# Key, value and query tiles in rows of their own, head sums and rotations one weight slab later

## The chip, the cores and the metric

One core of one Trainium2 chip runs the kernel. The metric is device microseconds of one execution. Before the change the median of three runs is 2245.8 us (2245.16 to 2245.82).

## The reference, cut to what matters

A two-layer backbone works on 512 latent tokens and 256 context tokens of width 1024. Each layer has a token-mixing part with three branches (attention, pooling, convolution) and a gated feed-forward part. The change touches only how the attention inputs are made. In short:

```python
ux = hx @ w_in[i]                                # queries, keys, values, pool, conv, gates
q = rope(rmsnorm(heads(ux[..., :512]), q_norm))  # 8 heads of 64
k = rope(rmsnorm(heads(ux[..., 512:640]), k_norm))   # 2 heads of 64, context rows without rope
v = ux[..., 640:768]
p = softmax(q * 64**-0.5 @ k.T); o = p @ v
```

In layer 0 context and latent tokens (768 columns) have queries; in layer 1 only the latent ones (512 columns), while keys and values need all 768.

## The kernel before, in words

All activations are held transposed, features on the 128 partitions and tokens along the row. A weight matrix comes in slabs of up to eight 128x128 blocks; `gemm` (L529) multiplies one slab into a PSUM bank pair, in three passes (high x high, low part of x, low part of w), since every operand is split into an fp32r high part and remainder. SP loads a slab into one of two raw buffers (L382), ScalarE rounds it (`rounds`, L893) into one of four ring places, GpSimd subtracts to get the low part (`split_run`, L425), and TensorE uses it. SP loads a slab only when the split two slabs earlier has ended. `result_of(s)` on ScalarE first rounds all slabs up to s + 3, and then waits for slab s's GEMM. Every engine has its instructions in one fixed order written out by hand; each waits on counting semaphores.

`A[0]` and `A[1]` are two PSUM places of 1024 columns for GEMM results, `B` a third for transposes and spreads, `OD` a fourth for rotations, with head sums beside it. `t1`, `t2`, `t3` are three rows of 800 columns in SBUF. `acc` is an accumulator of eight rows that isn't used while queries, keys and values are made.

The stage in question has six tiles of 128 features: k, v, q0, q1, q2, q3. Key and value are one `gemm_pair` (L555) that follows the normalised input block by block; each query tile is one slab. For a k or q tile:
- ScalarE squares the PSUM tile into `t1` (L1023) and copies it, scaled by the norm's gain, into `t2` (L1026), which frees the PSUM place;
- TensorE sums the squares per head and token (`head_sums`, L600, products of two columns) and multiplies `t2` by a rotation matrix into OD (`sums`, L583);
- VectorE multiplies by sine into `t3` (L1543), `t2` by cosine (L1545), and adds (L1547);
- for k alone, VectorE's variance (L1299, L1300), ScalarE's root (L940) and TensorE's spread of it over the features (L613, 24 products) come first, and then VectorE multiplies (L1552);
- ScalarE copies the tile as fp32r high part (L1036 for k, four half-tile copies; L1041 for q, two), and VectorE writes the remainders (L1559, L1564), the last of which is the event `tile`.

For v, ScalarE copies the tile into `t1` (L1016), TensorE transposes it in six products (L680), ScalarE copies the high part (L1020) and VectorE makes the remainder (L1534).

As all tiles share `t1` and `t2`, ScalarE waits for `tile` of the one before, ahead of each eviction:

```python
result_of(...)                       # L1012
if prev: act.wait_ge(*seen("tile", ly, prev))
```

On TensorE the GEMM of tile n comes before the products of tile n - 1 (`finish`). Behind q3 come the GEMM of the convolution's gate, the products of q3, and the GEMM of its value branch. ScalarE takes the root of all q variances (L940), then the tanh of the gate (L1050, with an ACT table load of its own), and VectorE multiplies it with the value branch (L1575). Only then are both places free for the attention scores (L726): VectorE takes the row maximum (L1585) and its negated, scaled copy (L1589), ScalarE the exponential (L1075), VectorE the division (L1599), TensorE the transposes (L736) and products with v (L757). Attention is the stage that follows, 80 units in both layers together.

Of the kernel before, what the change touches and what calls it, by code (L numbers as in the profile page):

```python
# [27 lines left out]
ACT = mybir.ActivationFunctionType  # L28
# [3 lines left out]
P = 128  # L32
# [88 lines left out]
def build(nc, io, known):  # L121
# [33 lines left out]
    with ctx:  # L155
# [115 lines left out]
        def at(w, c0, c1):  # L271
            return w[:, 256 + c0:256 + c1]
# [236 lines left out]
        def _(pe):  # L509
# [146 lines left out]
            for ly in range(LAYERS):  # L656
# [12 lines left out]
                    spread(0, "pre1", ly, "pre1")  # L669


                tiles = ["k", "v", "q0", "q1", "q2", "q3"]

                def finish(n):
                    c = full if n in "kv" else cols
                    if n == "v":
                        take("B", "vt", ly)
                        pe.wait_ge(*seen("vcopy", ly))
                        for k in range(6):
                            ins = nc.tensor.transpose(at(B, k * P, (k + 1) * P), t1[:, k * P:(k + 1) * P], ident)  # L680
                        ins.then_inc(*pe_done.up("vt", ly))
                    else:

                        pe.wait_ge(*seen("tsq", ly, n))
                        if "OD" in last_use:
                            pe.wait_ge(*seen("free", *last_use["OD"]))
                        col, per = (TOK["k"], 2) if n == "k" else (TOK["q"] + 2 * int(n[1]), HEADS)
                        head_sums(t1, c[0][0], col, per).then_inc(*pe_done.up("stat", ly, n))
                        sums(rot, t_cols(t2), c, ("free", "gemm", ly, n), "rot", ly, n, w="OD")
                        if n == "k":  # L690
                            spread(0, "k", ly, "k", heads=KV)

                for n, name in enumerate(tiles):
                    w = n % 2
                    take(w, "gemm", ly, name)
                    if name == "v":
                        s = s0 + S_KV
                        gemm_pair(A, [(s, s + 1, 4), (s + 2, s + 3, 4)], (hh, hl), high_ready, low_ready, full)
# [182 lines left out]
        def _(act):  # L881
# [113 lines left out]
            for ly in range(LAYERS):  # L995
# [10 lines left out]
                h_high(ly, "pre1", 0, 0)  # L1006


                prev = None
                for n, name in enumerate(["k", "v", "q0", "q1", "q2", "q3"]):  # L1010
                    w, l0 = A[n % 2], (0 if name in "kv" else lo)
                    result_of(s0 + (S_KV + 2, S_KV + 3, S_Q, S_Q + 1, S_Q + 2, S_Q + 3)[n])  # L1012
                    if prev:
                        act.wait_ge(*seen("tile", ly, prev))
                    if name == "v":
                        nc.scalar.activation(t1[:, 0:T], at(w, 0, T), ACT.Copy).then_inc(  # L1016
                            *act_out.up("free", "gemm", ly, name))
                        noted[("vcopy", ly)] = noted[("free", "gemm", ly, name)]
                        act.wait_ge(*seen("vt", ly))
                        nc.scalar.activation(vh[:].rearrange("p a b -> p (a b)"), at(B, 0, T),  # L1020
                                             ACT.Copy).then_inc(*act_hi.up("vh", ly))
                    else:
                        nc.scalar.activation(t1[:, l0:T], at(w, l0, T), ACT.Square).then_inc(  # L1023
                            *act_tmp.up("tsq", ly, name))
                        gcol = V_KN if name == "k" else V_QN
                        nc.scalar.activation(t2[:, l0:T], at(w, l0, T), ACT.Copy,  # L1026
                                             scale=vec[:, ly, gcol:gcol + 1]).then_inc(
                            *act_out.up("free", "gemm", ly, name))
                        if name == "k":
                            root("k", 2 * TT, ly, "k")  # L1030
                        act.wait_ge(*seen("roped", ly, name))
                        if name == "k":

                            for kv in range(KV):
                                for p in range(2):
                                    ins = nc.scalar.activation(kk[64 * p:64 * p + 64, 2 * kv, :],  # L1036
                                                               t2[64 * kv:64 * kv + 64, 0:T], ACT.Copy)
                        else:
                            j = int(name[1])
                            for p in range(2):  # L1040
                                ins = nc.scalar.activation(qs[64 * p:64 * p + 64, 2 * j + p, l0:T],  # L1041
                                                           t2[64 * p:64 * p + 64, l0:T], ACT.Copy)
                        ins.then_inc(*act_hi.up("hi", ly, name))
                    prev = name
# [241 lines left out]
        def _(dve):  # L1286
# [235 lines left out]
            for ly in range(LAYERS):  # L1522
# [4 lines left out]
                    normalise(ly, "pre1", 0, 0, 0)  # L1527


                for n, name in enumerate(["k", "v", "q0", "q1", "q2", "q3"]):  # L1530
                    l0 = 0 if name in "kv" else lo
                    if name == "v":
                        dve.wait_ge(*seen("vh", ly))
                        v.tensor_tensor(vl[:].rearrange("p a b -> p (a b)"), at(B, 0, T),  # L1534
                                        vh[:].rearrange("p a b -> p (a b)"), ALU.subtract).then_inc(
                            *dve_lo.up("free", "vt", ly))
                        noted[("tile", ly, "v")] = noted[("free", "vt", ly)]
                        continue
# [4 lines left out]
                    v.tensor_tensor(t3[:, l0:T], at(OD, l0, T), sin[:, l0:T], ALU.mult).then_inc(  # L1543
                        *dve_out.up("free", "rot", ly, name))
                    link(v.tensor_tensor(t2[:, l0:T], t2[:, l0:T], cos[:, l0:T], ALU.mult), dve_tmp)  # L1545
                    dve.wait_ge(*dve_out.ago())
                    link(v.tensor_tensor(t2[:, l0:T], t2[:, l0:T], t3[:, l0:T], ALU.add), dve_tmp,  # L1547
                         *(() if name == "k" else ("roped", ly, name)))
                    if name == "k":

                        dve.wait_ge(*seen("spread", ly, name))
                        link(v.tensor_tensor(t2[:, 0:T], t2[:, 0:T], at(B, 0, T), ALU.mult), dve_tmp,  # L1552
                             "roped", ly, name)
                        noted[("free", "spread", ly, name)] = noted[("roped", ly, name)]
                    dve.wait_ge(*seen("hi", ly, name))
                    for a in range(2):
                        if name == "k":
                            for p in range(2):
                                ins = v.tensor_tensor(kk[64 * p:64 * p + 64, 2 * a + 1, :], t2[64 * a:64 * a + 64, 0:T],  # L1559
                                                      kk[64 * a:64 * a + 64, 2 * a, :], ALU.subtract)  # L1560
                                ins.then_inc(*(dve_lo.up("tile", ly, name) if a and p else dve_lo.up()))
                        else:
                            j = int(name[1])
                            ins = v.tensor_tensor(qs[64 - 64 * a:128 - 64 * a, 2 * j + a, l0:T],  # L1564
                                                  t2[64 * a:64 * a + 64, l0:T],
                                                  qs[64 * a:64 * a + 64, 2 * j + a, l0:T], ALU.subtract)
                            ins.then_inc(*(dve_lo.up("tile", ly, name) if a else dve_lo.up()))

                noted[("stat", ly, "q")] = noted[("stat", ly, "q3")]
                t0 = lo // P  # L1570
                variance("q", t0 * HEADS, (TT - t0) * HEADS, HD, ly, "q")

                dve.wait_ge(*seen("free", "cgate", ly, 0))
                dve.wait_ge(used, s0 + S_CONV + 2)
# [404 lines left out]
```

## Time and profile before

| | |
|---|---|
| median of 3 runs | 2245.8 us (2245.16 to 2245.82) |
| the profiled execution, its own time | 2242.06 us |
| its span in the trace | 2240.3 us |
| busy: TensorE, VectorE, ScalarE, GpSimd | 2134.7, 1337.7, 794.9, 783.3 us |
| mean granted TensorE clock | 0.982 of full |
| instructions | 27947 |

The span runs from the first to the last instruction of the profiled execution; its own time is a little longer, and is compared with the other runs. Busy shares are means over stages with different limits, so a stage is read from its own stretch. Lines such as L529 are those of a helper that all GEMMs share. A number in brackets at the end of a row of the timeline is the idle time before it and what ended it. Granted clock 1.00 is 2.4 GHz, 0.50 is 1.2 GHz.

### The profile page before, as it was taken

The page shows a single profiled execution, that of the slowest core. Times are in us where ns is not written, and L with a number is a line of the kernel's source. Part 1 is how long each engine was busy: PE and PEld are TensorE (multiplying, and loading weights), DVE is VectorE, ACT ScalarE, POOL GpSimd, SP SyncE. Part 2 cuts the span into 40 slices and gives each one's busy share as a digit, 9 for nine tenths or more (in the row PEclk, how much of TensorE's full clock was granted, in tenths as well). Part 3 has the DMA queues.
Part 4 walks back from the last instruction along what each step waited for, and adds up shares of the span by engine and source line. Part 5 has one row for each costly group of instructions (what it writes and reads, how often), then busy time and mean ns, then how long its engine had stood idle before and what let it go on. Part 6 is the DMA issues. An engine that isn't in the chain of part 4 may idle for free.

```text
span 2240.3 us, 27947 instructions
## 1 busy us (share of the span) xinstructions
PE 2134.7 (95%) x11302; PEld 1807.4 (81%) x11302; DVE 1337.7 (60%) x1812; ACT 794.9 (35%) x1154; POOL 783.3 (35%) x359
## 2 busy tenths in 40 slices
PE   6889899999999999999999987899999999999997
PEld 6777788888888888888888876677867877888885
DVE  6459899856774587847616674798954353101113
ACT  2446711142324522223212344572234344222223
POOL 3220023232334433423323345103444555444442
PEclk9999999999999999999999989999999999999998
DMA  7110012123344134534323221102222332323321
GB/s 295 38 47 1 1 52 70 43 88 112 105 159 151 58 119 134 187 101 135 105 85 111 94 95 66 48 1 66 88 78 90 108 123 82 97 94 95 94 85 66
DMA packets 63200, 205.24 MB, mean 92 GB/s; under 512 B 7136, under 2 KB 8288, under 8 KB 62816
## 3 DMA queue, kind: packets, MB, share of 16 engines
q1 hardware_dynamic: 57744, 190.87, 26.2%
q10 hardware_dynamic: 5328, 12.59, 1.5%
q8 instruction: 90, 1.47, 0.3%
q14 instruction: 38, 0.31, 0.0%
HBM read 197.79 MB, written 5.64 MB: 91 GB/s over the span
## 4 chain that ended last, share of the span: by engine, by line
PE 78%; DVE 17%; ACT 2%; issue 1%; DMA 1%; POOL 1%; ACTq 0%; DVEq 0%
PE ps L529 70%; DVE conv_acc L1624 3%; DVE ps L1624 2%; DVE unit_stats L1585 2%; PE ps L555 2%; DVE pt1l L1605 1%; DVE probs L1599 1%; DVE pt0l L1605 1%; PE ps L736 1%; PE ps L592 1%; PE ps L573 1%; PE ps L613 1%; PE ps L583 1%; PE ps L757 1%; PE ps L600 1%
## 5 line engine op out<-in xcount | busy, mean ns | idle before, releaser
L425 POOL TENSOR_TENSOR w_l<-w_raw,w_h 128x1024 fp32r<-128x1024 f32 (+3 forms) x296 | 683.7, 2314 | 1305.7 <-ACT w_h L893 1305.4
L529 PE MATMUL ps<-h_h,w_h 128*128 128x512 f32 (+1 forms) x1296 | 430.4, 372 | 5.9 <-ACT t L1145 4.2
L529 PE MATMUL ps<-h_l,w_h 128*128 128x512 f32 (+1 forms) x1296 | 426.1, 369 | 0.0
L529 PE MATMUL ps<-h_h,w_l 128*128 128x512 f32 (+1 forms) x1296 | 425.3, 368 | 0.0
L893 ACT ACTIVATE w_h<-w_raw 128x1024 fp32r<-128x1024 f32 (+3 forms) x296 | 280.5, 950 | 212.2 <-PE ps L529 148.6
L529 PEld LDWEIGHTS ps<-h_h,w_h 128*128 128x128 f32 x1296 | 244.8, 190 | 55.8 <-ACT t L1145 6.6
L529 PEld LDWEIGHTS ps<-h_h,w_l 128*128 128x128 f32 x1296 | 245.7, 190 | 43.6
L529 PEld LDWEIGHTS ps<-h_l,w_h 128*128 128x128 f32 x1296 | 245.4, 189 | 42.9 <-issue 1.2
L1485 DVE CUSTOM_DVE_ANT_0 ps<-ada_raw,c_row 128x1024 f32<-128x1024 f32 x160 | 268.4, 1677 | 9.1 <-DMA ada_raw<-in_ada 4.1
L529 PE MATMUL ps<-f_h,w_h 128*128 128x258 f32 (+1 forms) x672 | 173.1, 339 | 0.9 <-DVE t L1810 0.9
L529 PE MATMUL ps<-f_h,w_l 128*128 128x258 f32 (+1 forms) x672 | 173.5, 340 | 0.0
L529 PE MATMUL ps<-f_l,w_h 128*128 128x258 f32 (+1 forms) x672 | 172.4, 338 | 0.0
L529 PE MATMUL ps<-mid_h,w_l 128*128 128x512 f32 (+1 forms) x528 | 160.7, 359 | 0.0
L529 PE MATMUL ps<-mid_h,w_h 128*128 128x512 f32 (+1 forms) x528 | 160.0, 357 | 0.1
L529 PE MATMUL ps<-mid_l,w_h 128*128 128x512 f32 (+1 forms) x528 | 159.1, 355 | 0.0
L1624 DVE SCALAR_TENSOR_TENSOR ps<-conv_in,vec,ps 128x512 f32<-128x512 f32 (+1 forms) x180 | 143.8, 845 | 2.1
L529 PEld LDWEIGHTS ps<-f_h,w_h 128*128 128x128 f32 x672 | 127.5, 190 | 16.1 <-DVE t L1810 1.2
L529 PEld LDWEIGHTS ps<-f_l,w_h 128*128 128x128 f32 x672 | 127.1, 189 | 14.6
L529 PEld LDWEIGHTS ps<-f_h,w_l 128*128 128x128 f32 x672 | 127.0, 189 | 14.6
L529 PEld LDWEIGHTS ps<-mid_h,w_h 128*128 128x128 f32 x528 | 99.4, 188 | 16.2 <-DVE acc L1835 0.4
L529 PEld LDWEIGHTS ps<-mid_l,w_h 128*128 128x128 f32 x528 | 99.2, 188 | 15.5
L529 PEld LDWEIGHTS ps<-mid_h,w_l 128*128 128x128 f32 x528 | 99.2, 188 | 14.7
(236 smaller groups left out, 3222.6 us busy)
## 6 DMA issues: line engine op xcount, KB each, us to landing
w_raw<-in_w SPq DMA_DIRECT2D x222, 512.0 KB, 3.6
ada_raw<-in_ada SPq DMA_DIRECT2D x80, 512.0 KB, 3.6
w_raw<-in_w SPq DMA_DIRECT2D x50, 256.0 KB, 3.2
ada_first<-in_ada SPq DMA_DIRECT2D x16, 512.0 KB, 6.7
w_raw<-in_w SPq DMA_DIRECT2D x16, 384.0 KB, 3.1
x<-in_x ACTq DMA_DIRECT2D x8, 384.0 KB, 17.6
x_again<-in_x ACTq DMA_DIRECT2D x8, 384.0 KB, 7.7
x_between<-x SPq DMA_DIRECT2D x8, 384.0 KB, 2.3
```

What stands on the lines that cost most here:

```text
L425: nc.gpsimd.tensor_tensor(wl[:, s % RING, 0:n], raw[:, s % RAW, 0:n], wh[:, s % RING, 0:n], ALU.subtract).then_inc(split, 1)
L529: ins = nc.tensor.matmul(at(out, c0, c1), w[:, s % RING, b * P:(b + 1) * P], m[:, kt, first + c0:first + c1], start=(kt == 0 and n == 0), ...
L555: ins = nc.tensor.matmul(at(out, c0, c1), w[:, s % RING, b * P:(b + 1) * P], m[:, k, first + c0:first + c1], start=(i == 0 and n == 0), st ...
L573: ins = nc.tensor.matmul(DD[:, 2 * k:2 * k + 2], ada_first[:, n % ADA_SLOTS, b * P:(b + 1) * P], silu_c[:, b, :], start=(b == 0), stop=(b ...
L583: ins = nc.tensor.matmul(at(B if w == "B" else OD, c0, c1), mat, src(c0, c1), start=True, stop=True)
L592: ins = nc.tensor.matmul(token_sum(kind, TOK[kind] + t, 1), src[:, t * P:(t + 1) * P], ones[:, 0:1], start=start and first, stop=stop and ...
L600: ins = nc.tensor.matmul(token_sum("q", c, 2), src[:, t * P:(t + 1) * P], blk[:, 0:P:HD], start=True, stop=True)
L893: nc.scalar.activation(wh[:, n % RING, 0:nb * P], raw[:, n % RAW, 0:nb * P], ACT.Copy).then_inc(*rounded.up())
L1485: link(v.tensor_tensor_reduce(out=scratch, in0=tile, in1=c_row[:, s, :], scale=1.0, scalar=0.0, op0=ALU.mult, op1=ALU.add, accum_out=mod[: ...
L1585: link(v.reduce_max(ust[:, 0, c:c + n], at(A[u % 2], 0, n * nk).rearrange("p (r k) -> p r k", k=nk), AX.X), dve_tmp)
L1605: v.tensor_tensor(key_rows(pl, us[u - 2]), by_key_tile(at(B, 0, nk * q_tiles(us[u - 2])), us[u - 2]), key_rows(ph, us[u - 2]), ALU.subtrac ...
L1624: return v.scalar_tensor_tensor(out=taps_of(ly, j), in0=src, scalar=w, in1=taps_of(ly, j), op0=ALU.mult, op1=ALU.add)
```

## The change

The tiles of key and query get rows of `acc` for squares, scaled copy and sine product (q1 uses `acc[:, 7]`, `t1`, `t2`), value one row. Key's result goes to `A[1]`, value's to `A[0]`. Value's copy out of PSUM moves from ScalarE to VectorE, ahead of key's rotation. On TensorE key's products come after q0's GEMM and its spread after q1's; the products of q0 to q2 come a slab later than before, those of q3 keep their place. ScalarE's evictions wait only for the tile whose rows they reuse. The q variance comes before the last rotation, and root and tanh come before q3's copies. The diff, cut to its core (the bodies of the rotation and remainders are as before, with the new rows):

```diff
+        tile_bank = {"k": 1, "v": 0, "q0": 0, "q1": 1, "q2": 0, "q3": 1}
+        tile_rows = {"k": (acc[:, 0], acc[:, 1], acc[:, 2]), "v": (acc[:, 3],), "q0": (acc[:, 4], acc[:, 5], acc[:, 6]),
+                     "q1": (acc[:, 7], t1, t2), "q2": (acc[:, 4], acc[:, 5], acc[:, 6]),
+                     "q3": (acc[:, 7], acc[:, 0], acc[:, 1])}
...
@@ TensorE
-                for n, name in enumerate(tiles):
-                    w = n % 2
-                    take(w, "gemm", ly, name)
-                    if name == "v":
...
-                    elif name != "k":
-                        gemm(A[w], [(s0 + S_Q + n - 2, 8)], hh, hl, cols)
-                    if n:
-                        finish(tiles[n - 1])
...
+                gemm_pair((A[1], A[0]), [(s, s + 1, 4), (s + 2, s + 3, 4)], (hh, hl), high_ready, low_ready, full)
+                q_slab("q0")
+                head_products("k")
+                take("B", "vt", ly)
+                pe.wait_ge(*seen("free", "gemm", ly, "v"))
+                for k in range(6):
+                    ins = nc.tensor.transpose(at(B, k * P, (k + 1) * P), tile_rows["v"][0][:, k * P:(k + 1) * P], ident)
+                ins.then_inc(*pe_done.up("vt", ly))
+                q_slab("q1")
+                spread(0, "k", ly, "k", heads=KV)
+                head_products("q0")
+                q_slab("q2")
+                head_products("q1")
+                q_slab("q3")
+                head_products("q2")
                 take(0, "cgate", ly, 0)
                 gemm(A[0], [(s0 + S_CONV, 8)], hh, hl, cols)
-                finish(tiles[-1])
+                head_products("q3")
...
@@ ScalarE
+                result_of(s0 + S_KV + 3)
+                evict("k", V_KN, 0)
+                result_of(s0 + S_Q)
+                evict("q0", V_QN, lo)
+                root("k", 2 * TT, ly, "k")
+                act.wait_ge(*seen("vt", ly))
...
+                result_of(s0 + S_Q + 1)
+                evict("q1", V_QN, lo)
+                act.wait_ge(*seen("roped", ly, "k"))
...
+                q_high("q0")
+                result_of(s0 + S_Q + 2)
+                act.wait_ge(*seen("tile", ly, "q0"))
+                evict("q2", V_QN, lo)
+                q_high("q1")
+                result_of(s0 + S_Q + 3)
+                act.wait_ge(*seen("tile", ly, "k"))
+                act.wait_ge(*seen("tile", ly, "q1"))
+                evict("q3", V_QN, lo)
+                q_high("q2")
+                result_of(s0 + S_CONV)
                 root("q", HEADS * TT, ly, "q", scale=1.0 / HD)
-
-                result_of(s0 + S_CONV)
-                act.wait_ge(*seen("stat", ly, "q3"))
                 nc.scalar.activation(t1[:, lo:T], at(A[0], lo, T), ACT.Tanh, scale=0.5).then_inc(
                     *act_out.up("free", "cgate", ly, 0))
+                q_high("q3")
                 result_of(s0 + S_CONV + 1)
...
@@ VectorE
+                    if name == "q3":
+                        variance("q", lo // P * HEADS, (TT - lo // P) * HEADS, HD, ly, "q")
...
+                dve.wait_ge(used, s0 + S_KV + 4)
+                v.tensor_copy(tile_rows["v"][0][:, 0:T], at(A[0], 0, T)).then_inc(*dve_out.up("free", "gemm", ly, "v"))
+                turn("k", 0)
+                dve.wait_ge(*seen("vh", ly))
...
+                dve.wait_ge(*seen("spread", ly, "k"))
...
+                turn("q0", lo)
+                dve.wait_ge(*seen("hi", ly, "k"))
...
+                q_low("q0")
+                for name in ("q1", "q2", "q3"):
+                    turn(name, lo)
+                    q_low(name)
```

## Rows read from the trace of the kernel before

**Rows 1.** The page: span, chain by engine, weight loads (count, size, us to landing).
```profile
span 2240.3 us, 27947 instructions
...
PE 78%; DVE 17%; ACT 2%; issue 1%; DMA 1%; POOL 1%; ACTq 0%; DVEq 0%
...
w_raw<-in_w SPq DMA_DIRECT2D x222, 512.0 KB, 3.6
```

**Rows 2.** Chain of waits, layer 0 (start us, us, what).
```profile
84.95 2.84 PE ps L613 x24
...
94.35 3.05 DVE k_split L1559
...
100.28 9.96 PE ps L529 x48
...
112.87 8.43 PE ps L529 x48
...
154.52 1.28 ACT L1050
...
158.67 1.36 DVE unit_stats L1589
...
160.14 1.09 ACT probs L1075 x2
```

**Rows 3.** Timeline of TensorE, layer 0 (start us, us, engine, line, operation, idle before).
```profile
78.67 1.57 PE L555 MATMUL ps<-h_l,w_h 128*128 128x256 f32 x8
...
99.44 0.85 PE L680 MATMUL ps<-const,t 128*128 128x128 f32 x6 [2.03 <-ACT t L1016]
...
156.68 2.29 PE L726 MATMUL ps<-k_split,q_split 128*128 128x256 f32 x8 [2.22 <-ACT t L1050]
```

**Rows 4.** Chain of waits, layer 1.
```profile
1391.34 0.79 PE ps L600 x8
...
1393.09 5.58 PE ps L529 x24
...
1427.99 1.09 ACT probs L1075 x2
```

**Rows 5.** Timeline of TensorE, layer 1.
```profile
1363.19 1.57 PE L555 MATMUL ps<-h_l,w_h 128*128 128x256 f32 x8
...
1369.07 1.53 PE L613 MATMUL ps<-const,token_rs 128*64 128x128 f32 x24 [0.86 <-ACT token_rs L940]
...
1383.05 1.51 PE L680 MATMUL ps<-const,t 128*128 128x128 f32 x6 [6.67 <-ACT t L1016]
...
1424.53 2.89 PE L726 MATMUL ps<-k_split,q_split 128*128 128x256 f32 x8 [2.95 <-ACT t L1050]
```

**Rows 6.** Windows of 1 us, layer 0: busy us by engine, then granted clock, DMA.
```profile
84.00:85.00 1.00, 0.14 (x3) 0.08 (x3) 0.81 (x3) 0.21 (x1) 0.00 (x0) 0.50 0.00 0
```

**Rows 7.** Timelines of VectorE, then ScalarE, both layers.
```profile
101.16 0.96 DVE L1534 TENSOR_TENSOR v_l<-ps,v_h 128x768 fp32r<-128x768 f32 x1 [2.77 <-ACT v_h L1020]
...
160.92 0.16 DVE L1589 SCALAR_TENSOR_TENSOR unit_stats<-unit_stats,token_rs 128x1 f32<-128x1 f32 x1
...
161.45 0.62 DVE L1599 TENSOR_SCALAR probs<-probs,unit_stats 128x768 f32<-128x768 f32 x1
...
1396.56 1.40 DVE L1564 TENSOR_TENSOR q_split<-t,q_split 64x512 fp32r<-64x512 f32 x2 [1.41 <-ACT q_split L1041]
...
88.87 3.41 ACT L1036 ACTIVATE k_split<-t 64x768 fp32r<-64x768 f32 x4 [4.07 <-DVE t L1552]
...
1398.05 0.60 ACT L1023 ACTIVATE t<-ps 128x512 f32<-128x512 f32 x1 [0.51 <-DVE q_split L1564]
```

**Rows 8.** Queue of SP, layer 1: weight loads (first issue, us, count).
```profile
1365.49 62.72 SPq L382 DMA_DIRECT2D w_raw<-in_w  x9
```

**Rows 9.** Timeline of GpSimd, layer 0.
```profile
93.44 3.14 POOL L425 TENSOR_TENSOR w_l<-w_raw,w_h 128x1024 fp32r<-128x1024 f32 x1 [14.58 <-ACT w_h L893]
...
157.65 2.36 POOL L425 TENSOR_TENSOR w_l<-w_raw,w_h 128x1024 fp32r<-128x1024 f32 x1 [0.73 <-ACT w_h L893]
```

More of the change, by code:

```diff
@@ L669, in _ @@
                     spread(0, "pre1", ly, "pre1")
[L672 to L691, printed above, removed]
@@ L693, in _, with q_slab @@
[L693 to L702 removed]
+                def q_slab(n):
+                    take(tile_bank[n], "gemm", ly, n)
+                    gemm(A[tile_bank[n]], [(s0 + S_Q + int(n[1]), 8)], hh, hl, cols)
@@ new lines, in head_products @@
+                def head_products(n):
+                    c = full if n == "k" else cols
+                    square, scaled, _ = tile_rows[n]
+                    pe.wait_ge(*seen("tsq", ly, n))
+                    if "OD" in last_use:
+                        pe.wait_ge(*seen("free", *last_use["OD"]))
+                    col, per = (TOK["k"], 2) if n == "k" else (TOK["q"] + 2 * int(n[1]), HEADS)
+                    head_sums(square, c[0][0], col, per).then_inc(*pe_done.up("stat", ly, n))
+                    sums(rot, t_cols(scaled), c, ("free", "gemm", ly, n), "rot", ly, n, w="OD")
@@ L1006, in _ @@
                 h_high(ly, "pre1", 0, 0)
[L1009 to L1044, printed above, removed]
@@ new lines, in evict @@
+                def evict(name, gain_col, l0):
+                    square, scaled, _ = tile_rows[name]
+                    w = A[tile_bank[name]]
+                    nc.scalar.activation(square[:, l0:T], at(w, l0, T), ACT.Square).then_inc(*act_tmp.up("tsq", ly, name))
+                    nc.scalar.activation(scaled[:, l0:T], at(w, l0, T), ACT.Copy,
+                                         scale=vec[:, ly, gain_col:gain_col + 1]).then_inc(
+                        *act_out.up("free", "gemm", ly, name))
@@ new lines, in q_high @@
+                def q_high(name):
+                    act.wait_ge(*seen("roped", ly, name))
+                    j, scaled = int(name[1]), tile_rows[name][1]
+                    for p in range(2):
+                        ins = nc.scalar.activation(qs[64 * p:64 * p + 64, 2 * j + p, lo:T],
+                                                   scaled[64 * p:64 * p + 64, lo:T], ACT.Copy)
+                    ins.then_inc(*act_hi.up("hi", ly, name))
+                result_of(s0 + S_KV + 3)
+                evict("k", V_KN, 0)
@@ L1527, in _, with turn @@
                     normalise(ly, "pre1", 0, 0, 0)
[L1530 to L1538, printed above, removed]
+                def turn(name, l0):
+                    _, scaled, other = tile_rows[name]
                     dve.wait_ge(*seen("rot", ly, name))
@@ L1546, in _, with q_low @@
                     dve.wait_ge(*dve_out.ago())
-                    link(v.tensor_tensor(t2[:, l0:T], t2[:, l0:T], t3[:, l0:T], ALU.add), dve_tmp,
+                    link(v.tensor_tensor(scaled[:, l0:T], scaled[:, l0:T], other[:, l0:T], ALU.add), dve_tmp,
                          *(() if name == "k" else ("roped", ly, name)))
[L1549 to L1554, printed above, removed]
+                def q_low(name):
@@ L1555, in _ @@
                     dve.wait_ge(*seen("hi", ly, name))
+                    j, scaled = int(name[1]), tile_rows[name][1]
                     for a in range(2):
[L1557 to L1567, printed above, removed]
@@ new lines, in _ @@
+                dve.wait_ge(*seen("spread", ly, "k"))
+                scaled = tile_rows["k"][1]
+                link(v.tensor_tensor(scaled[:, 0:T], scaled[:, 0:T], at(B, 0, T), ALU.mult), dve_tmp, "roped", ly, "k")
+                noted[("free", "spread", ly, "k")] = noted[("roped", ly, "k")]
+                turn("q0", lo)
+                dve.wait_ge(*seen("hi", ly, "k"))
+                for a in range(2):
+                    for p in range(2):
+                        ins = v.tensor_tensor(kk[64 * p:64 * p + 64, 2 * a + 1, :], scaled[64 * a:64 * a + 64, 0:T],
+                                              kk[64 * a:64 * a + 64, 2 * a, :], ALU.subtract)
+                        ins.then_inc(*(dve_lo.up("tile", ly, "k") if a and p else dve_lo.up()))
```

23 lines of the change are left out of this document (19 added, 4 removed).

## The prediction

> **What bounds the kernel now.** I read the page first. TensorE holds 78% of the chain that ended last, of a span of 2240.3 us [rows 1]. So the end moves when TensorE's idle or slow stretches go, and not when another engine does less. The diff touches one stage in each layer, from the end of the key/value GEMM pair to the first softmax exponential, so I followed the chain of waits through both copies of it, then TensorE's timeline there for its gaps.
>
> In layer 0 the pair ends at 78.67 + 1.57 = 80.24 [rows 3]. After it come key's head sums and rotation, the wait for key's root, and key's spread, which ends at 84.95 + 2.84 = 87.79 [rows 2]. Only then does query slab q0 start. After q0 TensorE idles 2.03 us until value's copy L1016 [rows 3]: ScalarE may write `t1` only when VectorE is through with key's tile, and VectorE's third key remainder took 3.05 us [rows 2]. Then the q slabs run back to back: a slab takes 8.43 us, and the slab at 100.28, which came behind that idle, 9.96; the products after it last from 110.24 to 112.87, 2.63 us [rows 2]. The value-branch GEMM ends at 156.68 - 2.22 = 154.46; the 2.22 us are the wait for the gate's tanh [rows 3], whose table load starts only at 154.52. The first exponential starts at 160.14 [rows 2].
>
> Layer 1 has the same shape with 512 columns: the pair ends at 1364.76, TensorE idles 6.67 us ahead of value's transposes and 2.95 ahead of the scores, so the last GEMM ends at 1421.58 [rows 5]; a slab takes 5.58, its products 1393.09 - 1391.34 = 1.75, and the exponential starts at 1427.99 [rows 4]. The extra time on a slab behind a gap is the clock: granted 0.50 (1.2 GHz) at 84 to 85 us, after head sums and rotations with short waits [rows 6], against full clock (2.4 GHz) in the steady slabs.
>
> **The change, part by part.**
>
> *Value's bank.* q0 now uses the bank of value, not of key. So it waits for value's PSUM-to-row copy, new on VectorE and ahead of key's rotation there. The trace has no such plain copy of 768 columns. The nearest are L1534 with a PSUM operand, 0.96 us, and L1599, SBUF to SBUF, 0.62 us [rows 7]. I take 0.96, since it reads PSUM, with 0.05 us on either side: 1.06 us in each layer. VectorE stands idle there, so nothing is queued behind it but key's rotation, which comes only after q0.
>
> *Key's products a slab later.* They no longer wait for an eviction: key's is done during q0's 8.43 or 5.58 us. They cost 2.63 us at full clock. Root and variance of key are hidden behind q1, so the spread has no wait and costs what it costs in layer 1, 1.53 us [rows 5], instead of 2.84 at the low clock. If that cover went, the waits of 0.86 us between products and spread would come back.
>
> *Value's copy and transposes.* The copy needs no tile of key any more, so the waits of 2.03 and 6.67 us go, and with them the slow slabs behind them. The transposes cost 0.85 [rows 3].
>
> *Weights.* Per slab, the rounding on ScalarE, the split on GpSimd and the load that SP issues are as before in number and order. Moved is the third rounding of the stage (slab S_KV+6), now ahead of key's eviction. In layer 1 its load is issued only when the split two slabs earlier ends, at 1365.49 [rows 8]; with the page's 3.6 us to landing [rows 1] it is there at 1369.1. Passes of 768 columns take 3.41 / 4 = 0.85 us by L1036 [rows 7], so one of 1024 some 1.1: it is rounded at 1370.2, and key's square and scaled copy end at 1371.0 and 1371.9. TensorE wants the first at 1364.8 + 1.06 + 5.58 = 1371.4 and the second after the head sums, so this costs nothing, by 0.4 us. In layer 0 the load was issued earlier and there is room.
>
> *Rows of their own.* Evictions no longer wait for the tile just before, but q2's still waits for the remainders of q0, which now stand behind all of key's. In layer 1, counted from the end of q1's GEMM: spread 1.53, multiply 0.96, key's four copies 3.41, its four remainders 3.84 (by L1534's 0.96 each), q0's two 1.40, q2's square 0.60, with one block by a split (2.1) 13.9 us [rows 7]. TensorE wants that square after spread, two products and two slabs: 1.53 + 2 x 1.75 + 2 x 5.58 = 16.2. So it costs nothing, by 2.3 us; in layer 0, with slabs of 8.43, there is more room. Later tiles take 1397.96 - 1393.09 = 4.9 us from rotation to last remainder [rows 4, 7] and 0.7 more to the end of the next square, 1398.65, and have two slabs for it.
>
> *Root and tanh ahead of copies.* Variance comes before the last rotation, root before the table load, tanh before q3's copies. The tanh ended 156.68 - 154.52 = 2.16 us after its table load began; with variance and root ahead (an estimate: at most as long again) that is 4.3 us beside a value-branch GEMM of 8.43 or 5.58. So the waits of 2.22 and 2.95 us go. What is late next is VectorE's gate product and the row maximum: in layer 0 158.67 - 156.68 = 1.99 us, then the negated maximum. That took 1.36 us [rows 2], since a GpSimd split ran until 160.01 [rows 9]; its next one takes 0.16 [rows 7]. The split now ends before it. With 0.05 and 0.11 us of issue the tail is 2.3 us in layer 0. In layer 1 the gate product is shorter, but the maximum needs the scores: half of the 2.29 us for two units [rows 3], 1.15, plus 1.0 for the maximum (half of 1.99), 0.16 and 0.11 gives 2.4.
>
> **The sum.** Layer 0, pair to last GEMM: 1.06 + 6 x 8.43 + 5 x 2.63 + 0.85 + 1.53 = 67.2, against 154.46 - 80.24 = 74.2: 7.0 less. Tail 2.3 against 5.7: 3.4 less. Layer 1: 1.06 + 6 x 5.58 + 2.63 + 4 x 1.75 + 0.85 + 1.53 = 46.6, against 56.8: 10.2 less. Tail 2.4 against 6.4: 4.0 less. Together 24.7 us (rounded terms add to 24.6). Attention starts that much earlier in each layer and is itself unchanged. The profiled execution took 2242.1 us (1.8 outside its span) and gives 2217.4; the median of the runs lies 3.7 above it, at 2245.8, so the forecast is 2221.1.
>
> **A rule against it.** The third key remainder started at 94.35 while a GpSimd split ran from 93.44 to 96.58; it ended at 97.40, so it did its 0.95 us after the split [rows 2, 9]. The gaps that the change removes ahead of value are partly this. In the new order other operations with both inputs in SBUF (rotation multiply and add, remainders) meet splits at new places; rival 1 prices that.
>
> The Trainium skill, in "SBUF — State Buffer", section "Who interferes with whom", says that a VectorE instruction with two SBUF inputs contends with a GpSimd one that reads SBUF, and the first to start holds the port for its whole length. By that rule, the trace agrees: 3.05 us for a 0.95 us instruction. Without it the sum is 2221.1, with it at the end of both stages rival 1's.
>
> **The rivals.**
> 1. *Blocked at the end (15%).* The split of the last slab before attention starts 1.1 us after q3's copies, about when the second of its two remainders does. Before, these started just ahead of the split. If the split is first, the remainder, gate product and maximum wait for it, up to 2.4 us [rows 9] a layer: 2225.9. Blocks further up eat the 2.3 us of slack in layer 1 before they cost TensorE anything. For: layer 1's remainders end within 0.2 us of its last GEMM. Against: the order on the two engines is the same as in the old steady slabs.
> 2. *The clock falls in thin stretches (12%).* Key's products and transposes now stand together (3.5 us), then spread and q0's products (4.2 us), and 1.06 us of idle comes ahead of q0. For: the 0.50 at 84 us. Against: layer 1's spread took 1.53 us behind the same products, so the clock stayed full there [rows 5], and so it did in the steady slabs of 8.43. A fall costs 9.96 - 8.43 = 1.5 us on a slab; at four places 6.1 us: 2227.2.
> 3. *Slower: the tile chain becomes the bound (3%).* Place: q2's eviction, which waits for q0's remainders behind key's, and each later one. It decides from 14.7 us per two slabs in layer 1 and 22.1 in layer 0. A tile's chain is 1.75 + 4.9 + 0.7 = 7.3 us in layer 1, some 11 in layer 0 (an estimate by the columns). If each of its five operations waited for a whole split of 3.14 us [rows 9], 23.0 and 26.7 would give 4.2 and 2.3 us more per slab, over six slabs 39 us, less the 24.7: 2260. Against: there is one split per slab, so five blocks per tile cannot be had.
> 4. *It does not arrive (4%).* If attention's first units wait for late tiles of q or for VectorE, only a fifth of it is left: near 2241, within 0.2% of 2245.8, about what a measurement of this kernel can tell from no change.
>
> **How the numbers follow.** My case has 66%. Its own range is 2217 to 2224: the copy at 0.62 and a shorter tail give a microsecond or two, the profile's lower time gives more, and lost slack takes up to 3. The high end adds rivals 1 and 2 together: 2221.1 + 4.8 + 6.1 = 2232. Low end 2216. Left out are rivals 3 and 4 and about 10% on the two sides. Faster by over 0.2% holds all but rivals 3 and 4: 93%; the same 4%; slower 3%.
>
> **What would show it.** TensorE's idle between pair and q0 near 1.1 us and none ahead of the transposes; spread 1.5 us in layer 0; granted clock full from pair to scores; no idle between last GEMM and scores; first exponentials near 149.7 and 1403 (1413.7 less layer 0's 10.4); first negated maximum 0.16 us. I am wrong if TensorE waits for ScalarE's square before a product, if the clock shows 0.50 between slabs, or if the last q remainder runs over 2 us.

## The result, and the profile after

The changed kernel takes 2218.6 us (median of four runs, 2217.3 to 2220.6) against 2245.8 (2245.2 to 2246.7) of the kernel before beside it: a ratio of 0.9879, 95% interval 0.9862 to 0.9896. Its profiled execution took 2219.4 us, with a span of 2217.6. The forecast was 2221.1, with 2216 to 2232 as its range.

One slip in what stands ahead of the prediction: the section on the change says that the products of q0 to q2 come a slab later than before. They don't; before, too, they stood behind the GEMM of the next query slab. Only key's products move (from ahead of q0's GEMM to behind it) and its spread (to behind q1's). The sum of the prediction counted them rightly.

The changed page: span, busy time of TensorE, and the share of each engine in the chain that ended last.

```profile
span 2217.6 us, 27943 instructions
...
PE 2129.1 (96%) x11302; PEld 1805.5 (81%) x11302; DVE 1340.1 (60%) x1814; ACT 793.2 (36%) x1152; POOL 784.1 (35%) x359
...
PE 78%; DVE 16%; ACT 2%; DMA 1%; issue 1%; POOL 1%; ACTq 0%; DVEq 0%; SPq 0%
```

Work is as before; the span is 22.7 us shorter. The chain of waits in layer 0 answers to [rows 2] (start us, us, what; L534 is the GEMM, L605 the head sums, L588 the rotation, L703 the transposes, L618 the spread):

```profile
80.61 0.97 DVE acc L1570
...
81.62 8.71 PE ps L534 x48
90.33 1.23 PE ps L605 x12
91.56 1.40 PE ps L588 x4
92.96 0.66 PE ps L703 x6
93.61 8.42 PE ps L534 x48
102.03 1.46 PE ps L618 x24
...
139.49 8.44 PE ps L534 x48
...
149.89 0.17 DVE unit_stats L1609
...
150.16 1.09 ACT probs L1089 x2
```

After the value copy L1570, everything down to the last GEMM is TensorE, one piece behind the other. The spread takes 1.46 us and the slab behind value's transposes 8.42; before they took 2.84 and 9.96 [rows 2]. The stage has no stretch at the lower clock.

Layer 1, the same view, answers to [rows 4]:

```profile
1355.08 0.97 DVE acc L1570
...
1356.09 5.85 PE ps L534 x24
...
1370.80 1.46 PE ps L618 x24
...
1396.22 5.59 PE ps L534 x24
...
1403.53 0.50 DVE unit_stats L1609
...
1404.14 1.09 ACT probs L1089 x2
```

**The measure used below** is the way from the end of the key/value pair to the start of the first exponential, read in each profile. It was 160.14 - 80.24 = 79.9 us in layer 0 and 63.2 in layer 1. It is 150.16 - 80.57 = 69.6 and 1404.14 - 1355.04 = 49.1. So the stage gives 10.3 + 14.1 = 24.4 us; the prediction said 24.7. For the changed kernel it repeats to 0.1 us: a second profile gave 69.6 and 49.1 again. The kernel before has one profile; its layer 0 held a fall of the clock behind the pair (granted 0.50 from 84 to 89 us); e9 below, without it, came out 2.8 us shorter than forecast. e2, which is the same up to its tail, shows that fall too, at the same place. Whole times do not repeat so well; the section on the clock has their spread.

### The profile page after: what moved, and what is told of

It is laid out like the page before. It is cut to its first block, busy times and chain, and to the rows that moved or that the text cites. A ratio compares the mean times of both kernels' runs of the same rounds, so it can differ in the third digit from the quotient of the medians.

```text
span 2217.6 us, 27943 instructions
## 1 busy us (share of the span) xinstructions
PE 2129.1 (96%) x11302; PEld 1805.5 (81%) x11302; DVE 1340.1 (60%) x1814; ACT 793.2 (36%) x1152; POOL 784.1 (35%) x359
## 4 chain that ended last, share of the span: by engine, by line
PE 78%; DVE 16%; ACT 2%; DMA 1%; issue 1%; POOL 1%; ACTq 0%; DVEq 0%; SPq 0%
PE ps L534 71%; DVE conv_acc L1644 3%; DVE ps L1644 2%; DVE unit_stats L1605 2%; PE ps L560 2%; DVE pt0l L1625 1%; DVE pt1l L1625 1%; DVE probs L1619 1%; PE ps L597 1%; PE ps L744 1%; PE ps L578 1%; DMA w_raw<-in_w 1%; PE ps L618 1%; PE ps L588 1%; POOL w_l L430 1%
## 5 line engine op out<-in xcount | busy, mean ns | idle before, releaser
L534 PE MATMUL ps<-h_h,w_h 128*128 128x512 f32 (+1 forms) x1296 | 427.9, 370 | 8.2 <-ACT t L1159 4.2
L534 PE MATMUL ps<-h_l,w_h 128*128 128x512 f32 (+1 forms) x1296 | 425.0, 368 | 0.0
L534 PE MATMUL ps<-h_h,w_l 128*128 128x512 f32 (+1 forms) x1296 | 424.6, 368 | 0.0
L534 PEld LDWEIGHTS ps<-h_h,w_h 128*128 128x128 f32 x1296 | 243.6, 189 | 58.4 <-ACT t L1159 6.6
L534 PEld LDWEIGHTS ps<-h_h,w_l 128*128 128x128 f32 x1296 | 244.7, 189 | 43.4
L534 PEld LDWEIGHTS ps<-h_l,w_h 128*128 128x128 f32 x1296 | 244.2, 188 | 42.1 <-issue 1.2
L534 PE MATMUL ps<-f_h,w_h 128*128 128x258 f32 (+1 forms) x672 | 173.1, 339 | 0.9 <-DVE t L1830 0.9
L534 PE MATMUL ps<-f_h,w_l 128*128 128x258 f32 (+1 forms) x672 | 173.5, 340 | 0.0
L534 PE MATMUL ps<-f_l,w_h 128*128 128x258 f32 (+1 forms) x672 | 172.4, 338 | 0.0
L534 PE MATMUL ps<-mid_h,w_l 128*128 128x512 f32 (+1 forms) x528 | 160.7, 359 | 0.0
L534 PE MATMUL ps<-mid_h,w_h 128*128 128x512 f32 (+1 forms) x528 | 160.0, 357 | 0.1
L534 PE MATMUL ps<-mid_l,w_h 128*128 128x512 f32 (+1 forms) x528 | 159.1, 355 | 0.0
L534 PEld LDWEIGHTS ps<-f_h,w_h 128*128 128x128 f32 x672 | 127.5, 190 | 16.2 <-DVE t L1830 1.2
L534 PEld LDWEIGHTS ps<-f_l,w_h 128*128 128x128 f32 x672 | 127.1, 189 | 14.7
L534 PEld LDWEIGHTS ps<-f_h,w_l 128*128 128x128 f32 x672 | 127.0, 189 | 14.6
L534 PEld LDWEIGHTS ps<-mid_h,w_h 128*128 128x128 f32 x528 | 99.4, 188 | 16.1 <-DVE acc L1855 0.4
L534 PEld LDWEIGHTS ps<-mid_l,w_h 128*128 128x128 f32 x528 | 99.3, 188 | 15.6
L534 PEld LDWEIGHTS ps<-mid_h,w_l 128*128 128x128 f32 x528 | 99.2, 188 | 14.7
```

The source lines that it names most:

```text
L534: ins = nc.tensor.matmul(at(out, c0, c1), w[:, s % RING, b * P:(b + 1) * P], m[:, kt, first + c0:first + c1], start=(kt == 0 and n == 0), ...
```

## The experiments

### The tail: e1 and e2

e1 puts the old order at the end of the stage back into the changed kernel, e2 puts the new one alone into the kernel before.

```diff
 e1, ScalarE (VectorE's variance goes behind q3's remainders)
+                q_high("q3")
+                root("q", HEADS * TT, ly, "q", scale=1.0 / HD)
                 result_of(s0 + S_CONV)
-                root("q", HEADS * TT, ly, "q", scale=1.0 / HD)
                 nc.scalar.activation(t1[:, lo:T], at(A[0], lo, T), ACT.Tanh, scale=0.5).then_inc(
                     *act_out.up("free", "cgate", ly, 0))
-                q_high("q3")
```

> The changed kernel with the old order at its end: q3's copies and remainders first, then variance, root, rounding and tanh. Theory (the chain root to tanh is on the path when it stands behind the copies, and hidden beside the value-branch GEMM when ahead): TensorE idles some 2.3 us ahead of the scores in layer 0 and 3.0 in layer 1, and the first negated maximum is blocked by a split again, so the first exponentials come 3.6 and 4.2 us later than in the changed kernel: about 7.8 us longer, near 2226.5. Rival (the tail is hidden anyway by VectorE's gate product and row maximum): under 2 us longer.

> The kernel before with this part alone: variance of q ahead of the last rotation, root and tanh ahead of q3's copies; rows and order of the rest as before. Theory (the parts are independent and add): 3.4 us less in layer 0; in layer 1 4.0 less, or 3.4 if a split blocks q3's rotation: 6.8 to 7.4 us below the kernel before, near 2238.7. Rival (the tail pays only once the earlier stalls are gone, since q3's remainders are late): under 3 us less.

e1 measured 73.0 and 53.2 us from pair to exponential: 3.4 and 4.1 more than the changed kernel, where 3.6 and 4.2 were expected. Its median is 2227.0 (2224.9 to 2228.0), and its ratio to the kernel before 0.9936, interval 0.9921 to 0.9951. e2 measured 76.5 and 59.6: 3.4 and 3.6 less than the kernel before. Its median is 2236.5 against 2241.2, 4.7 less, and its ratio 0.998, interval 0.9969 to 0.9992, which is 1.8 to 6.9 us: the whole time gives somewhat less than the stage. Read in the stage, the theory holds from both sides: the part is worth 7.0 to 7.5 us, with or without the rest of the change. The chain of waits of e1 in layer 1 shows where it sits:

```profile
1405.56 0.95 issue
1406.51 1.28 ACT L1064
...
1407.81 0.60 ACT t L1064
1408.41 0.04 issue
1408.46 0.98 PE ps L734 x4
...
1410.45 1.35 DVE unit_stats L1608
...
1411.91 1.09 ACT probs L1089 x2
```

The rounding (shown as 0.95 us of issue), the table load and the tanh all stand between copies and scores, and the negated maximum L1608 takes 1.35 us, where the next one takes 0.16: a split ran from 1409.43 to 1411.78.

### Value's row alone: e9

The transposes read the new row; every order stays.

```diff
-                    if prev:
+                    if prev and name != "v":
                         act.wait_ge(*seen("tile", ly, prev))
...
-                        nc.scalar.activation(t1[:, 0:T], at(w, 0, T), ACT.Copy).then_inc(
+                        nc.scalar.activation(acc[:, 3, 0:T], at(w, 0, T), ACT.Copy).then_inc(
```

> The kernel before with one row of the accumulator for value and no wait for key's tile ahead of its copy; the order of every engine as before. Theory (the wait for key's tile is what costs; own rows help without any new order): in layer 0 the copy ends near 94 us, so the 2.03 us of idle and the slow slab behind it (1.5) go, 3.7 with the faster transposes; in layer 1 ScalarE is through with key's copies and a rounding only at 1377.0, so 1.5 of the 6.67 us of idle stay and some 7 go with the slow slab: 10.7 less from pair to first exponential in both layers together (76.2 and 56.2), near 2230 to 2235. Rival (ScalarE's order holds the copy back as much as the row does): under 4 us less, and idle ahead of the transposes as before in layer 1.

Measured: 73.4 and 59.3 us, 6.5 and 3.9 less than the kernel before. The sum, 10.4, is near the expected 10.7, but by luck: neither layer is as expected (3.7 and 7.0). In layer 0, 2.8 us more went than forecast, and the clock did not fall there in this profile; key's spread took 1.53 us, not 2.84:

```profile
83.71 1.53 PE ps L613 x24
85.24 8.62 PE ps L529 x48
```

In layer 1 the idle ahead of the transposes shrank to 1.50 us as expected, and a new wait came 8 us later. The chain of waits there:

```profile
1365.49 3.03 DVE k_split L1559
...
1368.55 3.04 DVE k_split L1559
...
1371.63 0.97 DVE v_l L1534
...
1372.68 0.60 ACT t L1023
...
1373.33 1.05 PE ps L600 x8
```

q0's square L1023 still waits for the tile ahead of it, value's, whose remainder L1534 stands behind all of key's, and VectorE's last two key remainders were blocked by two GpSimd splits, 3.03 and 3.04 us each for 0.95. GpSimd's timeline of e9 has both:

```profile
1364.58 3.13 POOL L425 TENSOR_TENSOR w_l<-w_raw,w_h 128x1024 fp32r<-128x1024 f32 x1 [9.32 <-ACT w_h L893]
1368.07 2.71 POOL L425 TENSOR_TENSOR w_l<-w_raw,w_h 128x1024 fp32r<-128x1024 f32 x1 [0.36 <-ACT w_h L893]
```

TensorE idled 1.55 us ahead of q0's head sums, 0.8 of it while value's own remainder ran, and the clock fell behind it (granted 0.50 from 1375 to 1378 us). So value's own row is not enough in layer 1 with the old waits and the old order; which of the two is needed beside it, this run does not tell. The median, 2235.9 (2229.6 to 2239.5), is 0.9976 of the kernel before, interval 0.9967 to 0.9986, some 5 us: half of what the stage says. The profiled run of 2229.6 was the fastest of ten, so its 6.5 us in layer 0 may not stand for all ten.

### Key's products behind q0: e4 and e6

e4 is the changed kernel with key's products, root and spread ahead of q0. e6 is e4 with key's eviction and root ahead of the third weight rounding.

```diff
 e4, TensorE
+                head_products("k")
+                spread(0, "k", ly, "k", heads=KV)
                 q_slab("q0")
-                head_products("k")
 e6, ScalarE, on top of e4
-                result_of(s0 + S_KV + 3)
+                rounds(s0 + S_KV + 5)
+                act.wait_ge(used, s0 + S_KV + 4)
                 evict("k", V_KN, 0)
                 root("k", 2 * TT, ly, "k")
```

> The changed kernel with key's products, root and spread ahead of q0 again (rows and banks as in the changed kernel, all else in its order). Theory (q0's GEMM covers key's eviction, which stands behind the rounding of a slab whose load lands late in layer 1): 1.5 us longer in layer 0 (TensorE idles 1.6 ahead of the head sums and 0.9 ahead of the spread, less the 1.03 for value) and 4.2 in layer 1 (idle 4.5 and 0.9), and up to 4 more where the clock falls behind the idle: 5.7 to 9.7 longer, 7.5 likely, near 2226. Rival (own rows alone brought the gain, the order of key nothing): under 2 us longer.

> The kernel of e4 (key's products, root and spread ahead of q0) with key's eviction and root ahead of the stage's third weight rounding. Theory (what e4 lost in layer 1 was the weight slab's landing ahead of the eviction, and the low clock behind that idle; the cover of q0 itself is worth little): idle ahead of the head sums 0.9 us in both layers and 0.9 ahead of the spread, from pair to first exponential 70.3 and 49.8, 1.4 us more than in the changed kernel, and 2 to 3 more if the clock still falls. Rival (the products need q0 ahead of them whatever the eviction does): 56 us or more in layer 1.

e4 measured 71.3 and 58.5 us: 1.7 and 9.4 more than the changed kernel (median 2231.1, ratio to before 0.9953, 0.9936 to 0.9969). Layer 0 is near the 1.5 expected. In layer 1 the idle was the 4.5 us forecast, but the low clock behind it took more than the 4 us allowed for, so the 11.1 in all lie above the expected 5.7 to 9.7. TensorE's timeline of e4:

```profile
1359.98 2.72 PE L605 MATMUL ps<-const,acc 128*128 128x2 f32 x12 [4.49 <-ACT acc L1021]
1362.56 2.91 PE L588 MATMUL ps<-acc,const 128*128 128x256 f32 x4
1366.33 2.83 PE L618 MATMUL ps<-const,token_rs 128*64 128x128 f32 x24 [0.86 <-ACT token_rs L948]
```

These take about twice the 1.23, 1.40 and 1.46 us of the changed kernel. The square L1021 waited for a rounding, and that for its slab (`[5.89 <-DMA w_raw<-in_w]` stands behind it in ScalarE's timeline).

e6 measured 73.1 and 51.6: 3.5 and 2.5 more than the changed kernel, where 0.7 and 0.7 were expected and 2 to 3 in all on top if the clock fell. It fell in both layers, and 4.6 us went beside the forecast 1.4 (median 2223.1, 2219.5 to 2225.4; ratio 0.9914, 0.9899 to 0.9929). So the rival of e6 is refuted (51.6, not 56), but the theory's "the cover is worth little" is only half right. The chain of waits in layer 0:

```profile
80.45 1.50 PE ps L605 x12
81.95 2.24 PE ps L588 x4
...
85.03 2.83 PE ps L618 x24
87.86 9.26 PE ps L534 x48
```

With these products ahead of q0 TensorE has two waits of 0.9 us in a stretch of thin work, and the clock fell there. Behind q0 there is no wait, and it did not fall there in any profile of that order. The waits alone don't decide it: in layer 0 of e4 they were 1.8 and 0.9 us, and the clock stayed full.

### Value's copy on VectorE, and value's bank: e5, e3 and e7

e5 moves value's copy back to ScalarE, as its first instruction behind the rounding. e3 puts q0 into B instead of value's bank, so that it does not wait for the copy; e7 is e3 again.

```diff
 e3
-                    gemm(A[tile_bank[n]], [(s0 + S_Q + int(n[1]), 8)], hh, hl, cols)
+                    gemm(B if n == "q0" else A[tile_bank[n]], [(s0 + S_Q + int(n[1]), 8)], hh, hl, cols)
```

> The changed kernel with value's copy out of PSUM on ScalarE again (its first instruction behind the stage's third weight rounding), own row kept. Theory (the move to VectorE matters since ScalarE waits for a weight slab first): q0 starts 0.7 us later in layer 0 and 3.6 in layer 1, where the slab lands 2.7 us after the pair; with that idle of 4.6 us the clock may fall for up to 2.7 more: 4.3 to 7 us longer, from pair to first exponential 70.2 and 52.7 to 55.4. Rival (a copy is a copy): the same time.

> The changed kernel with q0's GEMM into the third PSUM place B in place of value's, so that it does not wait for VectorE's copy of value. Theory (the 1.06 us between pair and q0 in each layer are paid in full on the path): 2.1 us less than the changed kernel, near 2216.5, with no idle of TensorE between pair and q0. Rival (the transposes, which now wait for q0's eviction, give it back): no difference, and idle ahead of the transposes.

> The changed kernel with q0's GEMM in B, again, for a comparison with the changed kernel on the same chip. Theory: the way from pair to first exponential is 68.3 and 47.8 us as in the first run of it (changed kernel 69.6 and 49.1), and the median 2 to 3 us below that of the changed kernel. Rival (clock noise is all there was): the same time.

e5 measured 71.8 and 54.1 us: 2.2 and 5.0 more than the changed kernel, 7.3 in all against 4.3 to 7 expected (one run, 2229.7). ScalarE's timeline of e5 in layer 1 shows what the copy L1036 waits for; the pair ended at 1359.80:

```profile
1362.50 1.06 ACT L901 ACTIVATE w_h<-w_raw 128x1024 fp32r<-128x1024 f32 x1 [5.91 <-DMA w_raw<-in_w]
1363.46 0.79 ACT L1036 ACTIVATE acc<-ps 128x768 f32<-128x768 f32 x1
```

In layer 0 the move cost 0.7 us as expected, and q0's slab ran in 10.23 us instead of 8.7, at the lower clock behind an idle of 1.8; in layer 1 TensorE idled 4.51 us and the slab took 7.41 instead of 5.85.

e3 measured 68.3 and 47.8, e7 68.3 and 47.8: 1.3 less in each layer, where 1.06 was expected; the rest is that q0's first products are faster without a start behind an idle (8.43 against 8.71 us). TensorE's timeline of e3 at the seam:

```profile
77.86 1.57 PE L560 MATMUL ps<-h_l,w_h 128*128 128x256 f32 x8
79.27 0.52 PE L534 MATMUL ps<-h_h,w_h 128*128 128x256 f32 x2
```

Medians: e3 2216.9 (2211.8 to 2220.0), e7 2215.0 (2213.3 to 2217.1), the latter with 0.9864 of the kernel before (0.9849 to 0.9878), beside 0.9888 (0.9872 to 0.9905) for the changed kernel measured with it. That is 5.1 us below the changed kernel's median, where 2 to 3 were expected, but the intervals overlap. The stage is shorter by 2.6 us in both profiles; the version is the best one tried, by a difference in whole time that these runs don't separate.

### A split laid over the remainders: e8

```diff
                     *act_out.up("free", "cgate", ly, 0))
+                rounds(s0 + S_CONV + 1 + RING - 1)
                 q_high("q3")
```

> The changed kernel with the last rounding before attention moved ahead of q3's two copies, so that GpSimd's split of that slab runs when VectorE comes to q3's remainders. Theory (an operation of VectorE with both inputs in SBUF does not start while a split runs): the first remainder lasts to the split's end plus 0.7 to 0.95 us instead of 0.95 or 0.69, and the first exponential comes 0.3 to 0.8 us later in layer 0 and 1.7 in layer 1 (from the pair 70.0 to 70.4 and 50.8). Rival (no block; only ScalarE's order changes): the remainders keep 0.97 and 0.70 us each, and the first exponential moves by less than 0.5 us in layer 1.

Measured: 69.6 and 50.6 us (one run, 2219.0). Layer 0 does not move, where 0.3 to 0.8 were expected; layer 1 moves by 1.5. VectorE's timeline of e8, q3's two remainders in each layer:

```profile
145.22 2.58 DVE L1565 TENSOR_TENSOR q_split<-acc,q_split 64x768 fp32r<-64x768 f32 x2 [2.25 <-ACT q_split L1031]
...
1399.28 2.48 DVE L1565 TENSOR_TENSOR q_split<-acc,q_split 64x512 fp32r<-64x512 f32 x2 [2.35 <-ACT q_split L1031]
```

and GpSimd's:

```profile
143.61 2.40 POOL L430 TENSOR_TENSOR w_l<-w_raw,w_h 128x1024 fp32r<-128x1024 f32 x1 [6.40 <-ACT w_h L901]
...
1398.09 2.40 POOL L430 TENSOR_TENSOR w_l<-w_raw,w_h 128x1024 fp32r<-128x1024 f32 x1 [2.44 <-ACT w_h L901]
```

Unblocked they take 1.94 and 1.40. The split ended at 1400.49 and the first remainder could only start then. In layer 0 the split ended at 146.01, so the block cost 0.6 us, and 0.1 of slack was left. In layer 1 not all of the 1.5 us is the block. The rounding that the edit puts ahead of q3's copies makes the remainders start 0.9 us later behind the pair's end than in the changed kernel (1399.28 - 1353.02 = 46.3 against 1400.36 - 1355.04 = 45.3), which costs 0.8 at the gate product; the block adds 2.48 - 1.40 = 1.1, and the negated maximum, free this time, gives 0.3 back. This is rival 1 made on purpose: its mechanism is real, and in the changed kernel's own order it does not happen to the remainders.

### The same kernel again, and the clock

> The changed kernel once more, beside the kernel before. Theory (both vary from run to run with the share of time at the lower TensorE clock: the 17 runs of before gave 2236.1 to 2247.3 us at mean granted clocks of 0.985 to 0.977): the changed kernel between 2215 and 2222, the higher the lower its mean clock, some 24 us below the median of before in the same job and not 27. Rival (the first comparison was right): 27 us or more.

Measured: 2220.1 us (2218.0 to 2221.6) against 2245.8 (2242.2 to 2249.6) of the kernel before beside it, 25.7 less. The theory's range for the changed kernel held; its 24 against the rival's 27 is not decided by medians that vary so. Beside the experiments the kernel before had 37 more runs, from 2236.1 to 2249.6 us, median 2242.7. The table has both ends and the largest group by granted clock; the other 20 lie between:

| mean granted clock of the run | runs of before | time, us |
|---|---|---|
| 0.977 | 6 | 2244.4 to 2249.6 |
| 0.982 | 9 | 2238.1 to 2242.9 |
| 0.984, 0.985 | 2 | 2236.1, 2237.0 |

A straight line through the 37 gives 1.3 us for each 0.001. As a check: a mean lower by 0.001 is 0.002 of 2240 us, 4.5 us, at 1.2 instead of 2.4 GHz, which costs at most half of that, 2.2 us, and less where TensorE isn't the bound. The first four runs of before, 2245.2 to 2246.7, lie above the median of the 37. So the 27.2 us of the first medians hold some of this variation. The stage's 24.4 hold less of it, but not none: the one profile of before has the clock's falls of that execution in it.

The two first profiles show the same thing the other way. The stages gave 24.4 us, the spans only 22.7. Part of what was lost is in layer 1's key/value pair, ahead of the stage. Stretches of 2 us in the changed kernel (busy us by engine, then granted clock):

```profile
1346.00:1348.00 2.00, 1.78 (x7) 1.55 (x8) 0.24 (x1) 1.97 (x5) 1.76 (x1) 0.68 0.00 0
1348.00:1350.00 2.00, 2.00 (x8) 1.71 (x7) 0.00 (x0) 1.97 (x5) 1.91 (x2) 0.50 0.00 0
```

and the same work in the kernel before:

```profile
1358.00:1360.00 2.00, 2.00 (x13) 1.77 (x12) 0.00 (x0) 1.97 (x4) 1.96 (x2) 1.00 0.00 0
```

Eight products in 2 us against thirteen: the tail of the pair took 1355.04 - 1346.22 = 8.8 us from its last wait for `h_h`, against 1364.76 - 1357.47 = 7.3. Nothing in the change touches it. What moved is the time at which the stretch came; whether that is the cause, no run shows. In e1 and e8, which have the changed kernel's order here, the same tail took 7.3.

## Why the prediction was right

- **The bound.** Right. TensorE's idle and slow stretches were the terms, and they went: in neither layer does it wait between q0's first product and the last GEMM. From the pair to the last GEMM it took 67.4 and 46.8 us, forecast 67.2 and 46.6.
- **Value's bank.** Forecast 1.06 us, measured 1.05 in both layers; the copy took 0.96, like the PSUM row it was priced by. e3 took it away and got 1.3.
- **Value's wait.** Right. It is gone in both layers. e9 shows that the row for value alone doesn't give all of it in layer 1.
- **Key's products later.** Right in size: 2.63 us for the products and 1.46 for the spread, without a wait, forecast 2.63 and 1.53. With the cover gone, 1.7 and 9.4 us come back (e4), and still 6.0 in all when the eviction comes early (e6). The prediction priced a lost cover by the waits of 0.86 us alone; the clock took more there.
- **Weights.** The slab was rounded ahead of key's eviction and its landing was waited for, as forecast. The slack was 0.4 us in the forecast and 1361.9 - 1359.5 = 2.4 in this profile, since the load was issued 0.8 us ahead of the pair's end, not 0.7 behind it. Most of that is the slow tail of the pair, which ended 1.5 us later. In e1 and e8, where the tail took 7.3, the load came 0.73 behind the pair's end and 0.7 us of slack were left: the forecast was right, and it is a thin margin. In ScalarE's timeline of layer 1:

```profile
1357.76 1.06 ACT L901 ACTIVATE w_h<-w_raw 128x1024 fp32r<-128x1024 f32 x1 [5.92 <-DMA w_raw<-in_w]
1358.73 0.80 ACT L1021 ACTIVATE acc<-ps 128x768 f32<-128x768 f32 x1
```

- **Rows of their own.** q2's square ended at 1384.9 in layer 1 and was wanted at 1387.1: 2.2 us of slack against 2.3 forecast, with the one block that was counted. A second block fell on a query's cosine product and cost nothing. VectorE's timeline of layer 1:

```profile
1376.81 5.96 DVE L1585 TENSOR_TENSOR k_split<-acc,k_split 64x768 fp32r<-64x768 f32 x4 [0.48 <-ACT k_split L1048]
...
1384.84 0.68 DVE L1554 TENSOR_TENSOR t<-t,const 128x512 f32<-128x512 f32 x1
...
1389.71 2.18 DVE L1554 TENSOR_TENSOR acc<-acc,const 128x512 f32<-128x512 f32 x1
```

- **Root and tanh.** Tails of 2.24 and 2.34 us, forecast 2.3 and 2.4; e1 and e2 put the part at 7.5 and 7.0, forecast 7.4. In layer 1 the sum came out by luck. The forecast had half of two units' scores, the maximum and a free negated maximum on the path: 1.15 + 1.0 + 0.16. There the scores ran beside the gate product, and the path was gate product, maximum and a blocked negated maximum: 0.69 + 0.91 + 0.50.
- **The rivals.** 1 (blocked at the end) showed only as 0.50 instead of 0.17 us on the negated maximum in layer 1; e8 made it happen to the remainders, at 1.1 us in layer 1. 2 (the clock falls in thin stretches) did not come in either profile of the changed kernel, nor up to the last GEMM in those of e1 and e8. It did come in e6 and e5 in both layers and in e4 in layer 1, each time behind an idle, but not behind the longer idle of e4 in layer 0, so the runs give no rule for it. 3 and 4 had no sign. The rule of the Trainium skill ("SBUF — State Buffer", "Who interferes with whom"), that the first of the two instructions to start blocks the other for its length, agrees with e8, where a remainder waits 1.2 us for a split's end, and with the steady slabs, where a remainder that starts just ahead of a split keeps its 0.97.
- **The time.** The terms were right to 0.3 us in their sum. Against the medians the forecast is 2.5 us too high (27.2 us went), against the profiled executions 2.0 too low (2242.1 - 2219.4 = 22.7 went, forecast 2217.4). Both are of the size that the clock makes from run to run. That the median came out so near is partly luck: the medians of before in the other comparisons were 2241.2, 2241.3 and 2245.8.

Of the 24.4 us, 7.0 are the tail (e2), and value's row alone gives 10.4 (e9), of which 2.8 are the clock in layer 0. Key's products behind q0 are worth 6.0 when key's eviction keeps its old place (e6), 4.6 of it beyond the idle, with the low clock. If these parts add, which no run tests, 1 us is left for the rows of key and q0 themselves. The 11.1 of e4 are not a part of the gain: with key first, its eviction behind the slab's landing costs what it did not cost before the change.

## What to carry to other kernels

When the bound engine waits for a chain that runs over several engines in turn, look for a slab of its own work that can be put between the start of that chain and its end, and give the tiles rows of their own, so that the order can be chosen at all. Put first on each in-order engine what frees the bound engine (root and tanh here, 7 us), and the copies behind it. Judge a change of about 1% by the stretch that it touches in two or three profiles of both kernels, since the whole time of one kernel moved by 0.6% with the clock.

## What was unexpected of the hardware

- Whether the clock falls does not follow from what a thin stretch holds. With the same products behind the pair, it fell where the pair had ended at 79.55, 80.24 and 80.26 us (e6, before, e2), and not at 79.13 and 79.40 (e4, e9), though e4 had the longest idle there, 1.8 us. The difference was worth 2.8 us in e9. Five profiles in this order can be chance; e6 also had a fall ahead of the pair (0.50 from 62 to 65 us), which the other four had not. Why is left open here; no run moved the stretch alone.
- Two splits in a row can hold VectorE twice: a remainder of 0.95 us waited out one split, did its work, and the next one met the next split (3.03 and 3.04 us in e9).
